# One stationary tile for a head's high and low values: two passes over the probabilities in both attentions

## What is computed

```python
# swa_attention
prob = e / (jnp.sum(e, axis=-1, keepdims=True) + jnp.exp(sg - m))
o = jnp.einsum('bngrqk,bnkgd->bnqgrd', prob.astype(vb.dtype), vb)
...
# nsa_attention: compressed, selected, window
o_c = jnp.einsum('bgrcn,bngd->bcgrd', p_c.astype(v_cmp.dtype), v_cmp)
o_s = jnp.einsum('bgrcnl,bgcnld->bcgrd', p_s.astype(vs.dtype), vs)
o_w = jnp.einsum('bgrck,bkgd->bcgrd', p_w.astype(vw.dtype), vw)
o = gc[..., 0:1] * o_c + gc[..., 1:2] * o_s + gc[..., 2:3] * o_w
...
# neighbourhood_attention
return jnp.einsum('bhcqij,bicjhd->bcqhd', p, v_win)
```

## Time and profile before

| | us |
|---|---|
| median of 3 runs | 1293.91 |
| span of the profiled execution | 1293.9 |
| TensorE busy, of it | 1278.1 (99%) |
| VectorE busy | 802.8 (62%) |
| ScalarE busy | 635.7 (49%) |
| GpSimd busy | 155.7 (12%) |
| first attention, from the first scores to the last values | 52.4 to 235.7 |
| neighbourhood attention, likewise | 836.2 to 903.0 and on to 905 |

### The profile page before, as it was taken

One profiled execution on the slowest core, in us unless ns is written; L12 is line 12 of the kernel. 1 busy time (PEld: TensorE's weight loads), 2 busy tenths in 40 slices (PEclk: granted clock), 3 DMA queues, 4 the chain that ended last, 5 costly groups with the idle time before them and its releaser, 6 DMA issues.

```text
span 1293.9 us, 16698 instructions
## 1 busy us (share of the span) xinstructions
PE 1278.1 (99%) x6136; PEld 1063.6 (82%) x6136; DVE 802.8 (62%) x1559; ACT 635.7 (49%) x1243; POOL 155.7 (12%) x146
## 2 busy tenths in 40 slices
PE   9999999999999999999999999999999999999998
PEld 8888888878888888888778777889888888888887
DVE  6699799685655565346788886578644343344334
ACT  6787576454335343234555655476543252342344
POOL 0022120000110011001002101022311030110111
PEclk9999999999999999999999999999999999999999
DMA  8211110433332333322323212432333323232321
GB/s 276 82 50 42 33 42 17 164 87 91 91 104 76 112 98 98 97 92 77 110 90 105 74 58 59 127 107 83 93 94 98 92 81 114 82 111 86 105 90 66
DMA packets 64624, 118.20 MB, mean 91 GB/s; under 512 B 7712, under 2 KB 12192, under 8 KB 64288
## 3 DMA queue, kind: packets, MB, share of 16 engines
q1 hardware_dynamic: 62704, 112.86, 28.7%
q10 hardware_dynamic: 1840, 4.29, 1.1%
HBM read 115.02 MB, written 2.10 MB: 91 GB/s over the span
## 4 chain that ended last, share of the span: by engine, by line
PE 87%; DVE 7%; issue 2%; ACT 2%; DMA 1%; POOL 0%; SPq 0%; POOLq 0%; DVEq 0%; ACTq 0%
PE bank L581 26%; PE bank L583 26%; PE bank L582 25%; PE bank L801 2%; PE bank L681 1%; PE bank L683 1%; PE bank L682 1%; DVE pp L2156 1%; PE bank L787 1%; PE bank L788 1%; DVE wl L1985 1%; DVE ptl L2178 1%; DVE pp L2173 1%; DMA raw<-in_w_swa 1%; DVE qs L2072 1%
## 5 line engine op out<-in xcount | busy, mean ns | idle before, releaser
L1985 DVE TENSOR_TENSOR wl<-raw,wh 128x512 fp32r<-128x512 f32 (+2 forms) x360 | 266.0, 750 | 326.6 <-ACT wh L1291 326.0
L1291 ACT ACTIVATE wh<-raw 128x512 fp32r<-128x512 f32 (+1 forms) x398 | 242.3, 619 | 287.6 <-PE bank L583 274.7
L581 PE MATMUL bank<-AH,wh 128*128 128x512 f32 (+1 forms) x848 | 333.0, 393 | 2.7 <-DVE AL L1999 0.8
L583 PE MATMUL bank<-AH,wl 128*128 128x512 f32 (+1 forms) x848 | 328.9, 388 | 0.0
L582 PE MATMUL bank<-AL,wh 128*128 128x512 f32 (+1 forms) x848 | 326.7, 385 | 0.0
L581 PE MATMUL bank<-BH,wh 128*128 128x512 f32 x624 | 248.4, 398 | 0.0
L583 PE MATMUL bank<-BH,wl 128*128 128x512 f32 x624 | 245.1, 393 | 0.0
L582 PE MATMUL bank<-BL,wh 128*128 128x512 f32 x624 | 243.8, 391 | 0.0
L581 PEld LDWEIGHTS bank<-AH,wh 128*128 128x128 f32 x848 | 159.5, 188 | 36.5 <-issue 4.0
L583 PEld LDWEIGHTS bank<-AH,wl 128*128 128x128 f32 x848 | 159.2, 188 | 35.3
L582 PEld LDWEIGHTS bank<-AL,wh 128*128 128x128 f32 x848 | 159.4, 188 | 33.0 <-issue 0.2
(11 more groups left out here) (336 smaller groups left out, 1632.0 us busy)
## 6 DMA issues: line engine op xcount, KB each, us to landing
raw<-in_w_dn SPq DMA_DIRECT2D x104, 256.0 KB, 2.6
raw<-in_w_gu SPq DMA_DIRECT2D x88, 256.0 KB, 2.6
raw<-in_w_up SPq DMA_DIRECT2D x64, 256.0 KB, 2.6
raw<-in_w_nsa SPq DMA_DIRECT2D x16, 256.0 KB, 2.6
raw<-in_w_pg SPq DMA_DIRECT2D x16, 256.0 KB, 2.7
raw<-in_w_naq SPq DMA_DIRECT2D x16, 256.0 KB, 2.6
nbi<-in_na_bias ACTq DMA_DIRECT2D x8, 448.0 KB, 3.3
raw<-in_w_swa SPq DMA_DIRECT2D x10, 256.0 KB, 3.0
```

What stands on the lines that cost most here:

```text
L581: t.matmul(o, w, xh, start=start, stop=False, skip_group_check=skip)
L583: return t.matmul(o, wl, xh, start=False, stop=stop, skip_group_check=skip)
L1291: a.activation(W[i % NW].h[:, 0:n], RAW[i % NRAW][:, 0:n], ACT.Copy).then_inc(*s_wh.up(i))
L1985: v.tensor_tensor(w.l[:, 0:n], RAW[i % NRAW][:, 0:n], w.h[:, 0:n], ALU.subtract).then_inc(*s_wl.up(i))
```

## The change

For each block of keys the high and the low part of one head's values now stand side by side in one stationary tile of 128 columns. Two passes, the high and the low probabilities, give four products: the high values' on partitions 0 to 63, the low values' on 64 to 127 of the unit's bank. The two halves have to be added afterwards, across partitions: ScalarE copies one half to the other half's partitions in SBUF (`out_part`), VectorE adds the other half from the bank (`out_add`), and when both groups (or both heads) are in, `out_high` and `out_low` follow, now from SBUF. Each group has its own bank, so 16 units of the first attention close one where 8 did; the compressed values are multiplied once per group, with high and low probabilities stacked on 128 partitions. The values are written with one instruction per block on each engine where there were two, and the zeros are no longer set. The first two products behind each attention are issued together, all their passes for inputs 0 to 2 ahead of input 3 (`behind_last`). `FILL1` has two of its pieces in another place.

```diff
-         10: [("w_nsa", 11)], 11: [("w_o_swa", 0)], 12: [("w_nsa", 12), ("w_o_swa", 1)],
-         14: [("w_nsa", 13), ("w_o_swa", 2)], 15: [("w_nsa", 14)], 16: [("w_nsa", 15)], 18: [("w_o_swa", 3)],
+         10: [("w_nsa", 11)], 11: [("w_nsa", 12)], 12: [("w_o_swa", 0), ("w_nsa", 13)],
+         14: [("w_o_swa", 1), ("w_o_swa", 2)], 15: [("w_nsa", 14)], 16: [("w_nsa", 15)], 18: [("w_o_swa", 3)],
...
         def closes(u):
-            kind, j, g = unit(u)
-            return g == 1 and kind in ("swa", "wn")
+            return unit(u)[0] in ("swa", "wn")
...
# TensorE, values
-                    vh, vl = v(kb)
-                    m = triple(o, vh, pt.h[:, c:c + w], pt.l[:, c:c + w], vl, first and n == 0, last and n == 3, True)
+                    t.matmul(o, v(kb), pt.h[:, c:c + w], start=first and n == 0, stop=False, skip_group_check=True)
+                    m = t.matmul(o, v(kb), pt.l[:, c:c + w], start=False, stop=last and n == 3, skip_group_check=True)
...
+                if kind == "cmp" or kind == "sl" and g == 1:
+                    c = unit_of("cmp", j, 0)
+                    b, free = bank.take(ob)
+                    e.wait_ge(*free, s_tl.at((c, 0)), s_ql.at("vc"))
+                    m = t.matmul(b[:, :], VC[g][:, :], pct[:, :], start=True, stop=False, skip_group_check=True)
...
+            def behind_last(name, src, ready, key):
+                bs = [bank.take((key, c)) for c in range(2)]
+                pair = [weights(name, c) for c in range(2)]
+                for c in range(2):
+                    e.wait_ge(*bs[c][1])
+                    for k in range(3):
+                        e.wait_ge(ready(k))
+                        col = slice(P * k, P * k + P)
+                        triple(bs[c][0][:, :], pair[c][0].h[:, col], src[k].h, src[k].l, pair[c][0].l[:, col], k == 0, False)
+                e.wait_ge(ready(3))
...
# ScalarE
-                for g in range(2):
-                    m = a.activation(of_group(V1[b].h[:, :], g), of_group(bank.ap(("w_vtok1", b))[:, 0:384], g), ACT.Copy,
-                                     scale=rcol[:, b:b + 1])
+                a.activation(high_places(V1[b][:, :]), by_head(bank.ap(("w_vtok1", b))[:, 0:384]), ACT.Copy,
+                             scale=rcol[:, b:b + 1]).then_inc(*s_xh.up(("v1", b)))
...
+            def out_part(key, g, dst, ready, *free):
+                e.wait_ge(ready, *free)
+                a.activation(dst[half(g), :], bank.ap(key)[half(1 - g), :], ACT.Copy).then_inc(*s_cp.up(key))
+            def out_high(pair, src, dst, *free):
+                e.wait_ge(s_ad.at((*pair, 1)), *free)
+                a.activation(dst.h, src[:, :], ACT.Copy).then_inc(*s_xh.up(pair))
...
# VectorE
+            def out_add(key, g, dst):
+                e.wait_ge(s_cp.at(key))
+                v.tensor_tensor(dst[half(g), :], bank.ap(key)[half(g), :], dst[half(g), :], ALU.add).then_inc(*s_ad.up(key))
+                bank.read(key, (s_ad, key))
+            def out_low(pair, src, dst):
+                e.wait_ge(s_xh.at(pair))
+                v.tensor_tensor(dst.l, src[:, :], dst.h, ALU.subtract).then_inc(*s_xl.up(pair))
...
                 if s < N_UNITS:
                     soft1(s)
+                if s >= 3 and closes(s - 3):
+                    key = out_key(s - 3)
+                    out_add(key, key[3], out_sum(key))
+                if s >= 4 and closes(s - 4) and unit(s - 4)[2] == 1:
+                    pair = out_key(s - 4)[0:3]
+                    out_low(pair, out_sum(pair), out_pair(pair))
                 if 1 <= s <= N_UNITS:
                     norm1(s - 1)
```

143 lines of the change are left out of this document (71 added, 72 removed).

## The result

The changed kernel takes **1310.95 us** (median of 4, 1308.88 to 1311.57) where the kernel before took 1294.72 in the same set: **1.0118 of the time, 95% interval 1.0105 to 1.0131**. It is slower by 16 us. The prediction was 1297.3 with a range of 1287 to 1303: the sign was right, the size was not, and the time lies outside the range. The profiled execution has a span of 1308.9 us against 1293.9.

The account below looks back on a forecast made before the run. TensorE and VectorE were taken as matched, VectorE bounding 78.35 to 119 and 161.2 to 236, TensorE between. From 1293.9: -0.6 + 5.1 - 3.2 + 1.3 + 2.8 - 2.0 = +3.4, so 1297.3 us, range 1287 to 1303.

Parts of the forecast that it names:

- The third pass: Both attentions: removing it saves TensorE 19.4 us, 14.8 in the first; 512-column matmuls stay 0.23 us apart.
- The prices: VectorE: 0.67 us per addition, nothing extra for an `out_low` replacing a subtraction, +0.4 us for `VC`.
- The start: Copying the values in fewer, wider instructions closes the hole before the matmul at 54.04: 0.6 us earlier, bounds 0 and 0.7.
- 78 to 119: First attention up to unit 10's scores: VectorE is the bound; seven additions and small subtractions add 5.1 us.
- C: Rival, the port: new `out_low` of the first attention exposed to GpSimd's subtractions; three hits give 1300 us; chance 0.06.
- B: Rival: additions wait for ScalarE's copy, holding the division behind; decisive if over three after 119 do; 1302 us, chance 0.15.
- 119 to 161.2: First attention: TensorE the bound again, gets back 3.2 us, loses 1.3 to a new wait at unit 13's step.
- 161.2 to the end of the attention: First attention: VectorE the bound; additions, one more `out_low` and the division of unit 27 delayed at the end: +2.8 us.
- The neighbourhood attention: Second attention: TensorE loses 4.6 us of passes, VectorE gets four new `out_low`; -2.0 us, bounds 0 and -4.6.
- The rule on the port: VectorE instructions with two SBUF inputs contend with GpSimd reading SBUF, others not: new `out_low` exposed, `out_add` immune.
- D: Rival, the clock: new holes in the first attention lower TensorE's granted clock, 3.6 us at 0.59; 1299 us; chance 0.04.
- A: Rival: VectorE's lag is absorbed inside the first attention; 1282.3 us in full, chance 0.07; halfway 1290.6 us, chance 0.15.

Follow-up runs that it names:

- e8: Changed kernel with a third matmul per key block put back in both attentions, compressed units staying at two passes; 1320.40 us, ratio 1.0196.
- e7: Changed kernel with the first attention's additions and GpSimd's low parts of the weights there both cut to one column; 1293.74 us, ratio 0.9999.
- e5: Kernel before with the change only in the neighbourhood attention and the product behind it; 1294.84 us, ratio 0.9999.
- e6: Kernel before with seven 64x512 additions on VectorE that nobody reads, in units 3 to 7 and 9; 1300.92 us, ratio 1.0044.
- e3: Changed kernel with GpSimd's low parts of the weights in the first attention cut to one column; 1304.32 us, ratio 1.0071.
- e4: Changed kernel with matmuls whose results are unused put on TensorE where it waits, in both attentions; 1307.31 us, ratio 1.0102.
- e11: Changed kernel with two of the first attention's 16 additions, at steps 3 and 28, moved behind the normalization of their step; 1303.10 us, ratio 1.0063.

## Why the prediction was wrong

The steps by their parts:

1. **The third pass** has the steps that were said: in two passes, 512-column matmuls are 0.23 us apart at full clock. Right. The third pass put back into the changed kernel costs 9.5 us (e8), so it isn't free there; against the kernel before, what its going gives is spent by what came with it (e7).
2. **The prices** were right. Additions took 0.66 us each (4.59 for seven; 0.67 taken), `out_low` 0.60, `VC` +0.46 (+0.4).
3. **The start**: the hole before the output product at 54 is closed. From the scores of unit 0 to those of unit 1 all ten kernels with the changed local units need 13.53 to 13.55 us; the profiled execution of before needs 14.34, but e5 and e6, with the same work up to there, 13.85. So the -0.6 lies between 0.3 and 0.8.
4. **78 to 119** is where it failed. The sum was 7 x 0.67 + 0.4 = 5.1; those terms measured 5.05. The queue grew by 10.1 (52.12 for 42.02). **The step that failed is to take before's rows as fixed and add the new ones to them.** With every later start moved, three of the subtractions met GpSimd's (3.18 us; e3: 3.31), and three additions waited for ScalarE (1.66). Both were on my list as rivals C and B, with the wrong victims: C was priced for the new `out_low`, B for the additions after 119.
5. **119 to 161.2**: said -1.9, measured +3.1 (42.16 to 45.30 from the scores of unit 10 to those of unit 16). Up to 3.1 us are the matmuls at half clock from 130.1; without that fall the stretch is 42.8 (e4), still +0.6. The one new wait that was worked out, in the step of unit 13, is there: the addition at 159.53 stood 1.22 us. So did that of the step of unit 10 (2.48 us) and of unit 15 (1.30), which were not.
6. **161.2 to the end of the attention**: said +2.8, measured -0.6 up to the scores of unit 27 and +0.46 behind them, or +2.3 against the 613.7 of the kernels without a fall at 772. The end was read rightly (the division of unit 27 behind the addition of unit 25) and sized too small: 2.98 us of waits against 1.5 not covered; e11 gives 2.6 for it. The rest of the term was too large.
7. **The neighbourhood attention**: said -2.0, is worth -0.3 (e5). In e5 the gain is there at first: values of the third unit start 34.96 us behind the first scores, before 36.11. Behind that, where VectorE had 3.66 us of room and three `out_low` were counted with 1.9, the first of them was hit by GpSimd (874.4, 1.67 us in place of 0.68), TensorE then stood idle for 1.04 and 0.56 us, up to 876.7 and 879.0, and the first output product starts 68.32 us behind the first scores where it was 68.59. The term took the new rows at their own length alone, as that of 78 to 119 did.

**The rule on the port.** The prediction gave it without an exception that the page makes: an instruction with at most one input in SBUF is left alone only outside the modes that use both ports. Its own row needs that exception: the multiplications of unit 15 have one tile as input, and yet two of the four were stretched, to 1.24 and 1.41 us. In which mode they ran no run here shows. For `out_low`, `out_add` and the subtractions of keys and queries the rule came out as it was given.

**The rivals.** B happened: the condition was over three additions after 119 that wait, five did (136.4, 159.5, 174.0, 245.0, 252.9). It said 1302 and had 0.15. C happened with its three hits, elsewhere (and three more `qs` rows were hit later, at 147.4, 164.3 and 189.5, where before had one). D happened four times, not once; it had 0.04. A did not: at unit 10 nothing was absorbed. The larger error is that I gave them as alternatives to one another. They have one cause, VectorE late, and come together: +3.4 for the forecast, 4 to 6 by my own price for B, 3.2 for C (e3), 2 to 3.6 for D (e4). These overlap and must not be added up to the microsecond, but they make 13 to 16 us, and the measured difference is 16. That the sum comes out is no proof, since two of its terms were measured afterwards; by the prediction's own prices (1302, 1300 and 1299 against 1297.3) the three together would have given 1306.4, still 4.5 us short.

What stays open: the price of B apart from the falls of the clock that follow its holes, since every run that moved additions also changed the falls; and what the collisions cost the kernel before, without which the net price of C is not known for the whole attention.

## What to carry to other kernels

In a stretch where the engine that gets new work has nothing left, that work costs at least its full length, whatever the other engine loses: seven additions of 0.67 us cost 5.3 us in the kernel before as well, one collision included, under a TensorE that had all its passes. An instruction that waits for another engine's fresh result belongs behind whatever is ready in the same step; two of 16 in the wrong place cost some 7 us of the 16. And when an engine that runs without a gap gets later, look up what else runs beside it or waits for it at the new times: rivals that have one cause are to be priced on top of the forecast, not in its place.
